# Four gather slots and six weight buffers in place of five and four, in a two-layer decoder trunk

## The chip, the cores and the metric

The kernel runs on 1 core of one Trainium2 chip. The metric is the device time of one launch in microseconds (us); lower is better.

## The reference

Two layers of a decoder trunk in float32, for 256 prompt rows and 32 sample rows (8 sequences of 4). The model width is 1024.

```python
for l in range(2):
    h = rmsnorm(x) @ w_in[l]                   # 1024 -> 8192: u, v, GLU, q, three gates
    y_a = spatial_gate(gelu(u), gelu(v))       # chunks of 128, 8 groups
    y_b = silu(layernorm(conv31(glu)))         # causal depthwise conv, 31 taps
    y_m = mem_attend(q, mem_k, mem_v)          # 4 heads, 256 memory tokens; sample rows: per-sequence caches
    x += (sig(gA)*(y_a@w_o_a) + sig(gB)*(y_b@w_o_b) + sig(gM)*(y_m@w_o_m)) @ w_out
    x += peer(rmsnorm(x))
# peer: per token and each of 8 heads, top 16 of 16384 experts through product keys;
#   hid = gelu(x . u_tab[eid]);  y = sum over the 128 experts of gate * hid * v_tab[eid]
y = rmsnorm(x)
```

The expert part fetches, for each of 288 tokens and 2 layers, 128 rows of the u table and 128 rows of the v table by index.

## The kernel before

The work is cut into four portions m = 0 to 3, two to a layer: an even portion has the first 128 prompt rows, an odd one the other 128 prompt rows and the 32 sample rows. A portion is first mixed (everything up to the expert keys, `mixing(m)` on each engine) and then has its experts retrieved. Retrieval of portion m runs beside the mixing of portion m+1: each engine has one program order that alternates a unit of retrieval with the slice of mixing that `reach` allows after it. Portion 0 is mixed alone at the start (to about 300 us), portion 3 is retrieved alone at the end.

**Retrieval.** Its unit is the pair, t = 0 to 287: two indirect gathers, each of 128 rows of 8 KB (a u row and its v row side by side), so 2 MB to a pair. Eight pairs are a step (32 tokens, 4 heads), k = t % 8 is the pair's place in its step; two steps are a group. The queues do this for pair t:

- POOL: `gather(t)` (L359), both gathers, after it has waited until the values of pair t - SLOTS are done (`v_used`). There are SLOTS = 5 slots of two 1 MB buffers.
- DVE: `dots(t)` (L972), the two dot products with the u halves, 1.22 us each.
- ACT: one Gelu of two columns (L422, `gel`).
- DVE: work for later steps that is put between the dots and the diags of some pairs: the top-16 search of one half (`pick_half`, at k = 0 and k = 7), `pick_pairs` at k = 1, `pick_experts` at k = 2, `gates` at k = 4. Then `diags(t)` (L983).
- PE: `values(t)` (L1358), 8 matmuls with the v halves; its end is `v_used`.
- DVE: at k = 1 of every even step also `add_group` (L991), behind the diags.

**Weights and caches.** SP loads 264 pieces, nearly all 1 MB, in the one order of `ITEMS` into a ring of RING = 4 buffers; piece n waits until piece n - RING is used up. The order in an odd portion is glu 8, q 4, ck 8 (K cache of the eight sequences), va 4, cv 8 (V cache), mg 8, ua 4, mg 16, out 4, ffn, wq 4, keys; an even one has mk 4 and mv 4 behind glu and no ck and cv. PE reads them in that order: L1057 and L1063 the weights, L1207 the ck pieces, L1236 the cv pieces.

SP's program holds other transfers between the loads, with waits of their own, and what comes behind such a wait is not issued before it ends:

```python
if (kind, i) == (("va", 3), ("ck", 3))[p]:            # p = m % 2
    sp.wait_ge(S["pe_o"], at("pe_o", m, 4))           # the prompt rows' attention is done
    sp.wait_ge(kv_stored, 32 * (l + 1))
    sp.dma_start(phase[:, 2 * D:4 * D], rows_in[rows_l, :])    # L329
```

In the same way an odd portion has, ahead of its fifth piece (glu 4), a wait for the transposes at the start of that portion (L312 and the loads behind it), and both kinds have a wait for the spatial gate's LayerNorm behind mg 5 (L332).

The buffers take 2 x 5 x 8 KB and 4 x 8 KB of each partition, 112 KB in all.

Of the kernel before, what the change touches and what calls it, by code (L numbers as in the profile page):

```python
# [35 lines left out]
FIRST = [sum(STEPS[i % 2] for i in range(m)) for m in range(PORTIONS + 1)]  # L36
NSTEP = FIRST[PORTIONS]
PAIRS = 8
SLOTS = 5
SCORE_SLOTS = 10  # L40


# [17 lines left out]

ITEMS = [it for m in range(PORTIONS) for it in items(m)]
ITEM = {it: n for n, it in enumerate(ITEMS)}
RING = 4
WKIND = [("glu", 8), ("mk", 4), ("mv", 4), ("q", 4), ("va", 4), ("ua", 4), ("mg", 24), ("out", 4), ("wq", 4)]
WROW = {}
for _k, _c in WKIND:
# [27 lines left out]
def freed(m, kind, i):  # L94

    nt = len(TB[m % 2])
    name, k = {"glu": ("pe_glu", 2 * i + 2), "mk": ("pe_mk", 2 * i + 2), "mv": ("pe_mv", 2 * i + 2), "q": ("pe_q", 2 * i + 2),
               "ck": ("pe_sk", i + 1), "va": ("pe_va", nt * (i + 1)), "cv": ("pe_so", i + 1), "mg": ("pe_mg", 2 * i + 2),
               "ua": ("pe_ua", 2 * i + 2), "out": ("pe_out", nt * (i + 1)), "ffn": ("xfrow", nt), "wq": ("pe_wq", 2 * i + 2),
               "keys": ("pe_sc", STEPS[m % 2])}[kind]  # L100
    return name, at(name, m, k)
# [49 lines left out]
def build(nc, x_in, consts_in, mem_in, cache_in, state_in, w_in, small_in, rows_in, ffn_in, fing_in, ws_in, wss_in, bs_in,  # L151
          keys_in, uv_in, y_out, memk_out, memv_out, convp_out, convs_out, vn_out):
    with ExitStack() as ctx:
        def sb(name, shape, dt=F32):
            return ctx.enter_context(nc.sbuf_tensor(name, shape, dt))

        def sem(name):
            return ctx.enter_context(nc.semaphore(name))

        S = {name: sem("s_" + name) for name in tuple(PER) + RUN}  # L160
        w_landed = [sem(f"w_landed{i}") for i in range(RING)]
        uv_landed = [sem(f"uv_landed{i}") for i in range(SLOTS)]
        x_landed = [sem(f"x_landed{t}") for t in range(TILES)]
# [5 lines left out]

        uv_region = sb("uv", [P, 2 * SLOTS * 2 * D])  # L170
        uvbuf = [uv_region[:, 2 * D * i:2 * D * (i + 1)] for i in range(2 * SLOTS)]
        ring_region = sb("ring", [P, RING * 2 * D])
        ring = [ring_region[:, 2 * D * i:2 * D * (i + 1)] for i in range(RING)]

# [84 lines left out]
        def landed(m, kind, i):  # L259
            n = ITEM[m, kind, i]  # L260
            return w_landed[n % RING], 16 * (n // RING + 1)

        def buf(m, kind, i):
            return ring[ITEM[m, kind, i] % RING]

        @block.sync
        def _(sp):
            def load(m, kind, i):
                n = ITEM[m, kind, i]
                l = m // 2  # L270
                if n >= RING:
                    name, k = freed(*ITEMS[n - RING])
# [78 lines left out]
        def _(pool):  # L351
            def gather(t):
                s, k, b = t // PAIRS, t % PAIRS, t % SLOTS
                pool.wait_ge(S["ids"], s + 1)
                if t >= SLOTS:
                    pool.wait_ge(S["v_used"], t - SLOTS + 1)
                for i in range(2):
                    c = 16 * (s % 2) + 2 * k + i
                    nc.gpsimd.indirect_dma_start(  # L359
                        out=uvbuf[2 * b + i], out_offset=None, in_=uv_in,  # L360
                        in_offset=bass.IndirectOffsetOnAxis(ap=ids[:, c:c + 1], axis=0),
                    ).then_inc(uv_landed[b], 16)
# [1098 lines left out]
```

## Time and profile before

| what | value |
|---|---|
| median of 3 runs | 2566.31 us (2560.45 to 2570.62) |
| the profiled execution: time, span | 2567.09 us, 2564.9 us |
| busy share: PE, DVE, ACT, POOL | 75%, 66%, 25%, 26% |
| mean granted TensorE clock | 0.855 |
| bytes moved by DMA | 905.88 MB, mean 353 GB/s |
| of these, gathers and SP's queue | 604.02 MB and 299.90 MB |
| gathers, ring pieces | 576 and 264 |

How to read it: busy shares are means over stretches with different limits, so the windows (busy time of each engine, granted clock, share of time in which the 16 DMA engines were busy, GB/s) have to be read beside them. The span is that of one execution; the time of the same execution is 2.2 us longer.

### The profile page before, as it was taken

How to read it: one execution, taken by the hardware profiler on the slowest of the kernel's cores; microseconds unless marked ns; L12 is line 12 of the kernel's file. 1: busy time of each engine (PE TensorE's matmuls, PEld its weight loads, DVE VectorE, ACT ScalarE, POOL GpSimd, SP SyncE). 2: the span in 40 equal slices, each digit the busy share in tenths (PEclk: the TensorE clock that was granted, in tenths of full speed). 3: DMA queues.
4: the chain of work that ended last, by engine and by line, in shares of the span. 5: the costliest groups of instructions: out<-in, count | busy, mean ns of one | idle time of the engine just before them, and what ended most of it. 6: DMA issues, size and time to landing. Idle time of an engine off the chain costs nothing.

```text
span 2564.9 us, 31043 instructions
## 1 busy us (share of the span) xinstructions
PE 1936.3 (75%) x10696; PEld 1213.1 (47%) x10696; DVE 1684.3 (66%) x4711; ACT 648.4 (25%) x1185; POOL 661.8 (26%) x608
## 2 busy tenths in 40 slices
PE   8999767577989758977889757757898975545554
PEld 7889636235766406644557404523676641000010
DVE  4372257867645586788765675787664478888785
ACT  2112232122142314122334213211214231131110
POOL 0000031212222332323222342122311234443442
PEclk9999979788899969988899877878889987687767
DMA  7566699689789899999899999878878989999997
GB/s 269 198 247 223 254 407 366 253 341 383 294 328 370 349 422 402 407 416 368 340 421 415 421 421 388 333 293 341 352 289 329 368 318 422 421 420 420 411 410 299
DMA packets 127835, 905.88 MB, mean 353 GB/s; under 512 B 16112, under 2 KB 16576, under 8 KB 18368
## 3 DMA queue, kind: packets, MB, share of 16 engines
q0 software_dynamic: 82944, 604.02, 58.5%
q1 hardware_dynamic: 44736, 299.90, 30.0%
q8 instruction: 85, 1.39, 0.2%
q14 instruction: 70, 0.57, 0.1%
HBM read 895.75 MB, written 8.11 MB: 352 GB/s over the span
## 4 chain that ended last, share of the span: by engine, by line
PE 49%; DVE 21%; DMA 17%; issue 5%; DVEq 3%; ACT 3%; POOL 3%; POOLq 0%; ACTq 0%
PE bank L1057 25%; DMA uv<-uv_in,idx_u 13%; PE bank L1358 11%; PE bank L1063 8%; DVE uv L972 6%; DVE yB L671 3%; POOL uv L359 2%; DMA ring<-w_in 2%; DVE diag L983 2%; DMA ring<-cache_in 2%; DVE tmp_s L681 1%; DVE yB L686 1%; ACT L422 1%; DVEq L666 1%; DVE pick L943 1%
## 5 line engine op out<-in xcount | busy, mean ns | idle before, releaser
L1358 PE MATMUL bank<-uv,diag 128*32 128x512 f32 x2304 | 728.5, 766 | 473.7 <-DVE diag L983 464.6
L359 POOL DMA_INDIRECT uv<-uv_in,idx_u x576 | 617.8, 1073 | 1709.4 <-PE bank L1358 1419.0
L972 DVE CUSTOM_DVE_ANT_0 uv<-uv,xrep 128x1024 f32<-128x1024 f32 x576 | 681.8, 1221 | 112.9 <-DMA uv<-uv_in,idx_u 112.4
L1358 PEld LDWEIGHTS bank<-uv,diag 128*32 128x32 f32 x2304 | 134.8, 128 | 936.4 <-DVE diag L983 637.5
L1057 PEld LDWEIGHTS bank<-xnT,ring 128*128 128x128 f32 x4096 | 531.9, 196 | 94.9 <-issue 88.0
L1057 PE MATMUL bank<-xnT,ring 128*128 128x128 f32 (+1 forms) x4096 | 556.7, 295 | 10.7 <-ACT yMA L422 8.6
L422 ACT ACTIVATE pick<-pick 128x2 f32<-128x2 f32 (+1 forms) x324 | 69.6, 215 | 1152.5 <-DVE pick L972 1151.9
L422 ACT ACT_TABLE_LOAD x255 | 327.2, 1283 | 15.1 <-PE bank L1063 6.0
L671 DVE SCALAR_TENSOR_TENSOR yB<-ext_p,small,yB 128x128 f32<-128x128 f32 x960 | 282.8, 356 | 20.5 <-issue 1.4
L983 DVE TENSOR_SCALAR diag<-consts,pick 128x32 f32<-128x32 f32 x576 | 151.1, 317 | 63.0 <-ACT pick L422 57.4
L1057 PE MATMUL bank<-yMA,ring 128*128 128x128 f32 (+1 forms) x1024 | 137.2, 287 | 0.0
L1057 PEld LDWEIGHTS bank<-yMA,ring 128*128 128x128 f32 x1024 | 131.1, 191 | 0.0
L853 DVE TENSOR_TENSOR sg<-sg,bank 128x128 f32<-128x128 f32 (+1 forms) x64 | 19.5, 304 | 166.7 <-PE bank L1057 127.6
L422 ACT ACTIVATE sg<-bank 128x160 f32<-128x160 f32 (+1 forms) x128 | 36.8, 290 | 211.9 <-PE bank L1057 211.3
L1063 PE MATMUL bank<-ring,xnT 128*128 128x256 f32 (+1 forms) x384 | 88.9, 389 | 1.6 <-DMA ring<-w_in 1.0
L422 ACT ACTIVATE phase<-bank 128x256 f32<-128x256 f32 (+2 forms) x88 | 30.6, 348 | 227.3 <-PE bank L1063 116.0
L1063 PE MATMUL bank<-ring,merged 128*128 128x256 f32 (+1 forms) x384 | 87.0, 383 | 0.8 <-DVE merged L855 0.8
L1063 PEld LDWEIGHTS bank<-ring,xnT 128*128 128x128 f32 (+1 forms) x384 | 62.6, 167 | 31.5 <-issue 10.2
L1063 PEld LDWEIGHTS bank<-ring,merged 128*128 128x128 f32 (+1 forms) x384 | 61.1, 163 | 30.7 <-issue 12.9
L731 DVE TENSOR_TENSOR ext_p<-bank,sg 128x128 f32<-128x128 f32 x32 | 9.3, 291 | 95.4 <-PE bank L1057 95.4
L1057 PE MATMUL bank<-yB,ring 128*128 128x128 f32 (+1 forms) x512 | 68.6, 287 | 0.0
L612 ACT ACTIVATE xrep<-xnf 32x1024 f32<-32x1024 f32 x64 | 67.4, 1053 | 1.5
(151 smaller groups left out, 1470.6 us busy)
## 6 DMA issues: line engine op xcount, KB each, us to landing
ring<-w_in SPq DMA_DIRECT2D x224, 1024.0 KB, 8.8
ring<-cache_in SPq DMA_DIRECT2D x32, 1024.0 KB, 11.6
uv<-uv_in,idx_u POOLq DMA_INDIRECT x576, 12.6
phase<-rows_in SPq DMA_DIRECT2D x4, 1024.0 KB, 6.8
ring<-keys_in SPq DMA_DIRECT2D x4, 1024.0 KB, 8.9
ext_s<-state_in SPq DMA_DIRECT2D x2, 1088.0 KB, 11.0
convs_out<-ext_s SPq DMA_DIRECT2D x2, 1088.0 KB, 16.3
ext_s<-mem_in SPq DMA_DIRECT2D x2, 1024.0 KB, 14.7
```

The lines of the kernel that those rows point to most:

```text
L359: nc.gpsimd.indirect_dma_start(out=uvbuf[2 * b + i], out_offset=None, in_=uv_in, in_offset=bass.IndirectOffsetOnAxis(ap=ids[:, c:c + 1], a ...
L422: ins = nc.scalar.activation(out, in_, func, bias=bias, scale=scale, **({} if accum is None else {"accum_out": accum}))
L612: ins = nc.scalar.activation(xrep[gg % 2][32 * i:32 * (i + 1), :], xnf[1 if t == 2 else 0][r0:r0 + 32], ACT.Copy)
L666: dve.drain()
L671: ins = V.scalar_tensor_tensor(out=yB[:, c, 0:P], in0=ext_p[:, c, w:w + P], scalar=wconv[:, c, w:w + 1], in1=yB[:, c, 0:P], op0=ALU.mult, ...
L681: V.tensor_tensor(tmp_s[:, :, :, :], ext_s[:, :, :, w:w + DSEQ], wide, ALU.mult)
L686: ins = V.tensor_tensor(ys, tmp_s[:, :, :, :], ys, ALU.add)
L972: ins = V.tensor_tensor_reduce(out=u, in0=u, in1=xrep[gg % 2][:, :], scale=1.0, scalar=0.0, op0=ALU.mult, op1=ALU.add, accum_out=hid[:, c: ...
L983: ins = V.tensor_scalar(diag[:, t % 4, i], fold, gel[:, c:c + 1], gate[:, c:c + 1], ALU.mult, ALU.mult)
L1057: ins = MM(out, w[:, k, P * b:P * (b + 1)], rhs(k), start=k == 0, stop=k == KB - 1)
L1063: ins = MM(out, lhs(k), w[:, k, :], start=k == 0, stop=k == KB - 1)
L1358: ins = MM(vbank[gg % 2][32 * n:32 * (n + 1), :], diag[:, t % 4, i], uvbuf[2 * b + i][:, D + 512 * n:D + 512 * (n + 1)], start=first and i ...
```

## The change

SLOTS goes from 5 to 4, RING from 4 to 6. A slot has two buffers, so gathers have 8 buffers and ring pieces 6, and the sum stays at 14 buffers of 8 KB a partition. All waits that are counted from SLOTS and RING follow; no instruction is added, removed or put elsewhere in a queue. `gather(t + SLOTS)` stays where it was in POOL's program, so at each place it now fetches the pair one earlier.

```diff
-SLOTS = 5
+SLOTS = 4
...
-RING = 4
+RING = 6
```

## Rows read from the trace of the kernel before

**Rows 1.** The page, part 2: DMA busy tenths in 40 slices of 64 us.

```profile
DMA  7566699689789899999899999878878989999997
```

**Rows 2.** Waits, whole span: who for whom, us in total, times, longest.

```profile
POOL uv L359 <- PE bank L1358: 1419.0, 244, 18.3
...
DVE uv L972 <- DMA uv<-uv_in,idx_u: 112.4, 77, 7.4
...
PE bank L1207 <- DMA ring<-cache_in: 27.7, 7, 6.3
...
PE bank L1236 <- DMA ring<-cache_in: 14.0, 6, 3.7
```

**Rows 3.** Windows: length, busy PE PEld DVE ACT POOL, clock, DMA share, GB/s.

```profile
2064.00:2096.00 32.00, 31.23 (x246) 21.36 (x244) 22.12 (x63) 10.72 (x28) 11.54 (x10) 1.00 0.80 310
...
2112.00:2496.00 384.00, 209.35 (x602) 37.11 (x604) 312.04 (x831) 69.41 (x141) 163.02 (x150) 0.73 1.01 419
816.00:864.00 48.00, 41.12 (x202) 24.41 (x201) 27.25 (x72) 8.44 (x19) 10.11 (x10) 0.89 0.80 299
864.00:960.00 96.00, 58.78 (x283) 18.79 (x281) 69.08 (x186) 21.39 (x48) 37.48 (x34) 0.79 1.01 421
...
1280.00:1560.00 280.00, 208.37 (x1190) 118.02 (x1188) 184.83 (x500) 88.39 (x155) 88.08 (x83) 0.87 1.01 420
...
556.00:571.00 15.00, 5.69 (x28) 1.55 (x32) 14.18 (x36) 5.04 (x8) 3.55 (x4) 0.69 0.60 220
```

**Rows 4.** Timeline of PE, cv pieces of portion 1: start, us.

```profile
574.67 1.03 PE L1236 MATMUL bank<-ring,ext_s 128*32 128x256 f32 x12
578.20 1.56 PE L1236 MATMUL bank<-ring,ext_s 128*32 128x256 f32 x16 [2.50 <-DMA ring<-cache_in]
...
582.68 3.29 PE L1358 MATMUL bank<-uv,diag 128*32 128x512 f32 x8
585.97 1.07 PE L1236 MATMUL bank<-ring,ext_s 128*32 128x256 f32 x16
...
592.76 3.35 PE L1358 MATMUL bank<-uv,diag 128*32 128x512 f32 x8
596.04 2.44 PE L1057 MATMUL bank<-xnT,ring 128*128 128x160 f32 x16
...
622.30 3.63 PE L1358 MATMUL bank<-uv,diag 128*32 128x512 f32 x8 [6.57 <-DVE diag L983]
```

**Rows 5.** Timeline of PE, cv pieces of portion 3.

```profile
1782.53 1.03 PE L1236 MATMUL bank<-ring,ext_s 128*32 128x256 f32 x12
...
1801.37 2.44 PE L1057 MATMUL bank<-xnT,ring 128*128 128x160 f32 x16
```

**Rows 6.** Timeline of SP, at the ck pieces of portion 1.

```profile
487.94 0.33 SPq L329 DMA_DIRECT2D phase<-rows_in  x1
488.97 4.63 SPq L281 DMA_DIRECT2D ring<-cache_in  x4
```

**Rows 7.** Timelines of DVE and POOL in the last retrieval, from several windows.

```profile
2193.14 1.22 DVE L972 CUSTOM_DVE_ANT_0 uv<-uv,xrep 128x1024 f32<-128x1024 f32 x1 [0.49 <-DMA uv<-uv_in,idx_u]
...
2209.85 1.67 POOL L359 DMA_INDIRECT uv<-uv_in,idx_u  x1 [4.15 <-PE bank L1358]
...
2213.02 1.23 DVE L972 CUSTOM_DVE_ANT_0 uv<-uv,xrep 128x1024 f32<-128x1024 f32 x1 [1.25 <-DMA uv<-uv_in,idx_u]
...
2217.97 1.23 DVE L972 CUSTOM_DVE_ANT_0 uv<-uv,xrep 128x1024 f32<-128x1024 f32 x1 [1.67 <-DMA uv<-uv_in,idx_u]
...
2233.83 1.22 DVE L972 CUSTOM_DVE_ANT_0 uv<-uv,xrep 128x1024 f32<-128x1024 f32 x1 [1.32 <-DMA uv<-uv_in,idx_u]
...
2252.09 1.70 POOL L359 DMA_INDIRECT uv<-uv_in,idx_u  x1 [4.93 <-PE bank L1358]
```

**Rows 8.** POOL's gathers of 1848 to 1852 us, one pair, no other gather under way.

```profile
L359 POOL DMA_INDIRECT uv<-uv_in,idx_u x2: 933/934/936, 1850.2 to 1851.4; - x2
...
DMA to landing us min/median/max: 5.6/6.6/7.5
```

## The prediction

> **What bounds the kernel now.** I began with the page's DMA row [rows 1]. For most of the run the DMA engines are eight or nine tenths busy, but there are sevens and eights between, so neither transfers nor an engine bound all of it. Both kinds of buffer that change can bind only where somebody waits for what lands in them, so the waits came next [rows 2]. POOL waits 1419 us for PE, which means that the slots are nearly always full: that costs nothing as long as what has landed lies ready. Waits that do cost are few. DVE waits for gathered rows 112 us in 77 places, PE for ring pieces 27.7 us at the ck pieces (L1207) and 14.0 us at the cv pieces (L1236), in both odd portions together; for weights it hardly waits at all.
>
> The windows say where [rows 3]. In the last retrieval the DMA engines are full: 1.01 at 419 GB/s for 384 us, with PE busy 209 and DVE 312 of them. The same holds at the end of retrieval 0 (864 to 960 us) and for 280 us of retrieval 1. Before two of these stretches the engines had room: 0.80 at 816 to 864 and 0.80 at 2064 to 2096. So there are two regimes. Beside a mixing, PE and DVE set the pace and pieces of the ring can be late in bursts; once a mixing is done, a retrieval is bound by the pace at which pairs land.
>
> **The ring, 4 to 6.** Work out the cv place of portion 1 [rows 4]. PE has used cv 3 at 574.67 + 1.03 = 575.7, waits 2.50 us for cv 4, more for cv 5 and cv 7, and begins mg 0 at 596.04: 20.3 us. Its work in these is four pieces at 1.07, two values at 3.29 and 3.35, and two transposes with the wait ahead of them, 1.2 us: 12.1 us. From 556 to 571 the DMA engines were only 0.60 busy [rows 3], because PE stood on DVE and POOL and all buffers were full. Six buffers take in cv 4 and cv 5 there. The pieces behind them then take the places in the queue that cv 4 to cv 6 had: cv 6 is there at 578.2, when cv 4 was, and mg 0 by 586.0, when cv 6 was. The work of 12.1 us ends at 587.8, behind both, so mg 0 begins there: 8.2 us saved. In portion 3 the same stretch takes from 1783.56 to 1801.37, 17.8 us [rows 5]; with the same work 5.7 us are saved. Together 13.9 us. After these places PE's slice of mixing is what DVE waits for, so I let the gain stand to the end of each mixing.
>
> At the ck place nothing is gained, although the waits are twice as long. SP stands at L329 behind ck 3 until 487.94, with two empty buffers under the change; then come the rows_in transfer and ck 4 to ck 7 from 488.97 [rows 6]. Now ck 4 would be issued some 0.7 us sooner, but behind the same rows_in, in the same queue, at the same share of full engines. Between 0 and 1 us; I take 0. If SP's wait were not there, it would be up to 27.7 us [rows 2]. The opening (portion 0 alone) has no ring wait either: 0. Other transfers of SP, behind its waits at glu 4, L329 and L332, are tied to other engines' work and keep their times, plus the shift.
>
> **The slots, 5 to 4, beside a mixing.** A gather is issued when a slot comes free, as before, so the traffic is the same at the same times, but it carries the pair one earlier: every pair lands one pair's turn later than it did. There DVE takes up a pair about every 9 us (64 of them from some 330 to 900 us) and hardly waits for a gather, so what has landed covers it. Without that cover it would cost a turn once, about 9 us. I take 0.
>
> **The slots in the three stretches that gathers bound.** The pace is one pair in 4.95 us (2213.02 to 2217.97) [rows 7], which is 2.1 MB at 419 GB/s [rows 3].
>
> *Entry.* Where such a stretch begins with all slots full, one pair less has landed, and it must be fetched at full engines: 5 us once. At 864 and at 2096 us the engines had had room before, so the two ring pieces that were fetched instead don't make up for it: SP keeps two pieces further ahead through retrieval 0's end, and at the last one nothing follows. 5 us each. In retrieval 1 the engines are full from 1280 on, and there the ring brings its 2 MB into the stretch and stops at glu 3 of portion 3 as before (the wait ahead of glu 4), so it asks for 2 MB less within it. These cancel: 0, with 5 as the bound.
>
> *Round trips.* With four slots the gather that POOL issues when pair t is done is pair t+4. The tight one is k = 2, behind pick_pairs and pick_experts. In an odd step, pair k = 1 is taken up at 2193.14 and the gather behind pair k = 2 is issued at 2209.85: 16.7 us. It must now bring the pair that is due five paces after k = 1, 24.8 us, so it has 8.1 us to land. In an even step add_group lies between as well: 2233.83 to 2252.09 is 18.3 us, which leaves 6.5 us [rows 7]. A pair alone lands 8.7 us after its first issue (1851.4 + 7.5 less 1850.2) [rows 8]. So the stream slips by 0.6 us in an odd step and 2.2 in an even one. The other pairs of a step have the room: they come free 5 to 10 us after they land, of four paces' 19.8. The last retrieval has about four odd and five even such steps with picking: 4 x 0.6 + 5 x 2.2 = 13.4 us. Retrieval 0's end has one odd step, 0.6; retrieval 1's end I put at 2.
>
> The landing time under the change is the unknown. Its lower bound is the first gather of the lone pair, 5.6, plus the 1.2 us between the two issues, as if only the bytes counted: 6.8, and then the slips are 0 and 0.3, 1.5 us in all. Its upper bound adds a slow issue (1.67 against 0.93 us, rows 7 and 8) to each half: 10.2, slips of 2.1 and 3.7, 27 us. I take 8.7, since it is the same transfer with nothing ahead, and nothing ahead is what a late issue means.
>
> **Sum.** Entry 10.0, last retrieval 13.4, ends of retrievals 0 and 1 2.6, ring -13.9: +12.1 us. The profiled execution took 2567.1 us, 0.8 above the median of three, so 2579.2 on its scale and 2578.4 against the median. I say 2578 us. No change, within 0.5% (about what a measurement of this kernel can tell), is 2553.5 to 2579.1, so my number lies just inside its edge.
>
> **The rivals.**
>
> - *The round trips hide.* If a pair that is issued while the one before it still moves lands in the 6.8 us of the lower bound, only the entries cost: 10.0 + 1.5 + 1 - 13.9 = -1.4, 2565 us. For it: in the dense stretches most of a gather's time is queueing. Against it: lone pairs take 8.7 in every case that I looked at, and an overlap of 2 us would have to come from somewhere. The Trainium skill's page "DMA: Bandwidth & Descriptors", section "Anatomy of one DMA — SWDGE (gpsimd) path", fits a transfer as about 2.0 us plus its bytes at 436 GB/s; as an estimate that is 6.8 us for a pair's 2.1 MB and speaks for this rival, while the trace's lone pair takes 8.7, and the measurement decides.
> - *The ring gain is given back.* Some 10 us behind each cv place PE stands 6.57 us for DVE's diag [rows 4]. If DVE is late there for reasons of its own (picks beside POOL's LayerNorm), the earlier PE only waits longer. Then +26.0: 2592 us. Against it: DVE's slices ahead of that diag wait for mg 0 and mg 1 themselves.
> - *The ring gains at ck too, on the other side.* If gathers with a slot less leave the engines to SP's queue behind 488 us, ck 4 to ck 7 and va 0 land as fast as PE takes them, and the 27.7 us go as well: -15.6, 2551 us. It decides once ck 4 lands as soon as PE is through with ck 3, a few us behind 488.97 [rows 6]. Against it: gathers are issued at the same moments with four slots as with five.
>
> **Chances.** My forecast 0.58, its own range 2569 to 2588, half of it on each side of 2579; hidden round trips 0.16; gain given back 0.14; gain at ck 0.12. Faster by over 0.5% (below 2553.5) comes from the last and a little of the first rival: 0.13. Within 0.5%: 0.29 + 0.15: 0.44. Slower: 0.29 + 0.14: 0.43. The range leaves out most of the ck case and the upper end of the costliest trips: 2554 to 2595.
>
> **What would show it.** In the profile after, the cv row of PE's waits (14.0) should fall to a few us and the ck row (27.7) stay; mg 0 of portion 1 should begin 6 to 9 us sooner. In the last retrieval the DMA share should fall below 1, to about 0.97, at some 406 GB/s, with DVE's waits for uv up in the pairs behind k = 2, above all in even steps; the stretch from 2112 us on should be 18 us longer. At the ends of retrievals 0 and 1 the DMA share stays near 1. I am wrong if the last retrieval keeps 419 GB/s (first rival), if PE's longer waits for the diag eat the cv gain (second), or if the ck waits shrink (third). A starved gather beside a mixing, with DVE waiting for uv there, would be a cost that I have not counted.

## The result and the profile after

The kernel with four slots and six ring buffers took 2576.64 us (median of 20 runs, 2566.11 to 2586.43), the kernel before 2564.27 us beside it (20 runs, 2556.35 to 2573.69). The ratio is 1.0056, 95% interval 1.0044 to 1.0068: slower by 12.4 us in the medians, 14 us by the ratio.

The profiled execution of after took 2570.7 us, 6 below its median; that of before lies 3 above its own. So the two traces differ by 3.4 us of span where the medians differ by 12.4, and a place by place account has to find the other 9 us as luck of these two executions. It does, further down.

The page of after: the span, the DMA busy tenths in 40 slices (before: [rows 1]), the uv queue's bytes and DVE's dots.

```profile
span 2568.3 us, 31044 instructions
...
DMA  7476598699889999988999999779988789999997
...
q0 software_dynamic: 82944, 604.02, 58.4%
...
L972 DVE CUSTOM_DVE_ANT_0 uv<-uv,xrep 128x1024 f32<-128x1024 f32 x576 | 681.9, 1221 | 146.1 <-DMA uv<-uv_in,idx_u 145.4
```

The waits of after over the whole span, which answer to [rows 2].

```profile
POOL uv L359 <- PE bank L1358: 1456.1, 246, 18.3
...
DVE uv L972 <- DMA uv<-uv_in,idx_u: 145.4, 80, 7.5
...
PE bank L1207 <- DMA ring<-cache_in: 26.5, 7, 6.3
...
PE bank L1236 <- DMA ring<-cache_in: 0.7, 1, 0.7
```

The two kinds of buffer show in two rows. The wait for cv pieces is gone (14.0 to 0.7), that for ck pieces is as it was (27.7 and 26.5), and DVE waits 33 us longer for gathered rows, in about as many places: the single waits got longer.

Windows of after, the same stretches as in [rows 3] where they answer to them (length, busy PE, PEld, DVE, ACT, POOL, granted clock, DMA share, GB/s).

```profile
864.00:960.00 96.00, 51.05 (x212) 9.94 (x203) 65.19 (x177) 21.32 (x45) 36.92 (x33) 0.75 1.00 410
...
1280.00:1560.00 280.00, 208.66 (x1173) 116.39 (x1171) 184.11 (x497) 88.24 (x154) 86.53 (x82) 0.87 1.00 412
...
2112.00:2496.00 384.00, 211.37 (x580) 36.80 (x578) 297.34 (x793) 65.83 (x134) 158.14 (x144) 0.69 0.98 398
...
571.00:608.00 37.00, 30.43 (x250) 21.95 (x240) 32.35 (x78) 9.30 (x16) 18.82 (x12) 0.99 1.01 413
```

The last retrieval is the plain one: 419 GB/s before, 398 now, over the same 384 us of the clock; its gathers are the same in number and size, so they take longer. The last row is the stretch of the last cv pieces of portion 1 and of mg behind them; in the kernel before it read as follows.

```profile
571.00:608.00 37.00, 29.17 (x219) 16.13 (x212) 22.02 (x76) 4.52 (x9) 6.02 (x7) 0.85 1.00 411
```

PE's timeline of after at the cv pieces of portion 1, which answers to [rows 4].

```profile
578.87 1.07 PE L1236 MATMUL bank<-ring,ext_s 128*32 128x256 f32 x16 [0.75 <-DMA ring<-cache_in]
...
580.80 1.91 PE L1358 MATMUL bank<-uv,diag 128*32 128x512 f32 x8
583.12 2.44 PE L1057 MATMUL bank<-xnT,ring 128*128 128x160 f32 x16 [0.41 <-DMA ring<-w_in]
```

mg 0 begins at 583.12 in place of 596.04. In portion 3 it begins at 1789.59 in place of 1801.37 [rows 5]:

```profile
1789.59 2.44 PE L1057 MATMUL bank<-xnT,ring 128*128 128x160 f32 x16
```

How a slip looks. DVE's dots of after in an even step of the last retrieval (two rows are a pair; those shown are first halves, but for the one at 2425.66), and then POOL's gathers of the same step.

```profile
2396.04 1.23 DVE L972 CUSTOM_DVE_ANT_0 uv<-uv,xrep 128x1024 f32<-128x1024 f32 x1 [0.38 <-DMA uv<-uv_in,idx_u]
...
2403.78 1.23 DVE L972 CUSTOM_DVE_ANT_0 uv<-uv,xrep 128x1024 f32<-128x1024 f32 x1
...
2416.59 1.23 DVE L972 CUSTOM_DVE_ANT_0 uv<-uv,xrep 128x1024 f32<-128x1024 f32 x1 [0.32 <-DMA uv<-uv_in,idx_u]
...
2424.51 1.23 DVE L972 CUSTOM_DVE_ANT_0 uv<-uv,xrep 128x1024 f32<-128x1024 f32 x1 [4.64 <-DMA uv<-uv_in,idx_u]
2425.66 1.22 DVE L972 CUSTOM_DVE_ANT_0 uv<-uv,xrep 128x1024 f32<-128x1024 f32 x1
2429.47 1.22 DVE L972 CUSTOM_DVE_ANT_0 uv<-uv,xrep 128x1024 f32<-128x1024 f32 x1 [1.80 <-DMA uv<-uv_in,idx_u]
```

```profile
2406.32 0.94 POOL L359 DMA_INDIRECT uv<-uv_in,idx_u  x1 [3.98 <-PE bank L1358]
...
2414.23 1.80 POOL L359 DMA_INDIRECT uv<-uv_in,idx_u  x1 [5.57 <-PE bank L1358]
2416.34 0.94 POOL L359 DMA_INDIRECT uv<-uv_in,idx_u  x1 [0.31 <-issue]
```

Pair k = 1 is taken up at 2396.04. The gather behind pair k = 2 goes out at 2414.23, 18.2 us later (18.3 in the kernel before [rows 7]), and it carries pair k = 6. Pairs 5, 6 and 7 are taken up at 2416.59, 2424.51 and 2429.47: 7.9 us and then 4.96. One gap of 7.9 where the pace is 4.95 is a slip of 3.0 us, and DVE's wait in it is 4.64 where the other waits of the step are under 2. Behind it the pairs come at the pace again, and the 3.0 us stay.

Both traces can be laid over each other by the starts of the dots, pair by pair. After less before, in us, and what changed over each stretch (an ordinary table, worked out from the L972 rows):

```
place                                     difference   change
opening                                       -1.9      -1.9
cv place of portion 1                        -12.2     -10.3
entry into retrieval 0's end                  -7.5      +4.6
its odd step (+1.6), and just behind (+0.6)   -5.3      +2.2
beside the mixing of portion 2, 1100-1115     -2.0      +3.3
retrieval 1's end (+4.8 on the way)           -1.9      +0.1
cv place of portion 3                        -12.2     -10.3
the mixing behind it                         -18.9      -6.7
entry into the last retrieval                -13.8      +5.1
slips of the last retrieval                   +3.8     +17.6
```

Two changes have no edit behind them: the opening's -1.9, where both kernels issue the same work, and the -6.7 behind the second cv place, where PE's granted clock was 0.81 in the kernel before and 0.90 after over the same 84 us (1820 to 1904). Without these two the table sums to +12.3, the medians' +12.4. The opening is luck of the execution of before: wide54 below, which is the kernel before in everything but the last retrieval, starts its dots 1.5 us ahead of it too. That the -6.7 is luck as well is shown only in part, and the table of places at the end of the experiments says how far. So the agreement to 0.1 us is closer than this account can carry.

### The profile page after: what moved, and what is told of

Read it like the earlier page. It is cut to its first block, busy times and chain, and to the rows that moved or that the text cites. A ratio compares the mean times of both kernels' runs of the same rounds, so it can differ in the third digit from the quotient of the medians.

```text
span 2568.3 us, 31044 instructions
## 1 busy us (share of the span) xinstructions
PE 1935.0 (75%) x10696; PEld 1208.8 (47%) x10696; DVE 1682.8 (66%) x4711; ACT 648.5 (25%) x1185; POOL 666.2 (26%) x608
## 4 chain that ended last, share of the span: by engine, by line
PE 49%; DVE 21%; DMA 16%; issue 5%; DVEq 3%; ACT 3%; POOL 3%; POOLq 0%; ACTq 0%
PE bank L1057 25%; DMA uv<-uv_in,idx_u 13%; PE bank L1358 12%; PE bank L1063 8%; DVE uv L972 7%; DVE yB L671 3%; DMA ring<-w_in 3%; POOL uv L359 3%; DVE diag L983 2%; DVE tmp_s L681 1%; DVE yB L686 1%; ACT L422 1%; DVEq L666 1%; DVE pick L943 1%; PE bank L1288 1%
## 5 line engine op out<-in xcount | busy, mean ns | idle before, releaser
L1358 PE MATMUL bank<-uv,diag 128*32 128x512 f32 x2304 | 737.8, 775 | 495.4 <-DVE diag L983 486.7
L972 DVE CUSTOM_DVE_ANT_0 uv<-uv,xrep 128x1024 f32<-128x1024 f32 x576 | 681.9, 1221 | 146.1 <-DMA uv<-uv_in,idx_u 145.4
## 6 DMA issues: line engine op xcount, KB each, us to landing
ring<-cache_in SPq DMA_DIRECT2D x32, 1024.0 KB, 17.6
uv<-uv_in,idx_u POOLq DMA_INDIRECT x576, 10.4
```

The source lines that it names most:

```text
L972: ins = V.tensor_tensor_reduce(out=u, in0=u, in1=xrep[gg % 2][:, :], scale=1.0, scalar=0.0, op0=ALU.mult, op1=ALU.add, accum_out=hid[:, c: ...
L1358: ins = MM(vbank[gg % 2][32 * n:32 * (n + 1), :], diag[:, t % 4, i], uvbuf[2 * b + i][:, D + 512 * n:D + 512 * (n + 1)], start=first and i ...
```

## The experiments

The theory to be tested: the change is a gain from the ring at the cv places (about 20 us in both portions), and a loss from the slots, most of it round trips in the last retrieval (about 16 to 18 us) besides the entries (about 10). The rivals: the loss lies elsewhere, the ring gave little, or the ck place stays because of memory traffic and not because of SP's order. All ratios are to the kernel before, whose median was 2565.3 us beside s4r4, hold46, ck46 and wide46 and 2565.8 us beside the other four (23 runs each). s4r4 was run 4 times, hold46, s4r5 and wideck46 6 times, the others 12 times.

**s4r4: the slots alone.** Four slots, and the ring as it was.

```diff
-SLOTS = 5
+SLOTS = 4
```

> Slots alone: 4 slots, 4 ring buffers, so the loss without the ring's gain. My theory, with the sizes of the changed kernel's profile: about 33 us for the slots (entry of retrieval 0's end 4.6, its even step 2.2, a starved gather in the mixing beside retrieval 1 3.3, last retrieval 22.7) and 5 more, since the ring no longer makes up for the entry of retrieval 1's end: 38 us, ratio to the kernel before 1.0145. Rival, the ring gives nothing and the slots cost all of the 12 us that were measured: 1.005.

Measured: 2601.6 us, ratio 1.0135 (1.0118 to 1.0153). The slot costs some 35 us, and from there to after's 1.0056 the ring gives back 0.0079, 20 us. For four slots with four ring buffers the prediction's terms make 31 us: 26.0, and the 5 us that it let the ring cancel at the end of retrieval 1. That term is real (+4.1 here, about 0 in after), so the ring's 20 us stand against 13.9 + 5. The slots were put 4 us too low and the ring 1 us. PE's wait at the cv pieces is back, and the last retrieval reads as in after:

```profile
PE bank L1236 <- DMA ring<-cache_in: 16.8, 8, 3.9
```

```profile
2112.00:2496.00 384.00, 209.94 (x578) 36.10 (x576) 295.48 (x788) 67.93 (x136) 160.99 (x147) 0.71 0.98 397
```

**hold46: four slots, six ring buffers, but cache pieces come no earlier than with four.** SP waits for the item four before, for ck and cv pieces only.

```diff
-                    name, k = freed(*ITEMS[n - RING])
+                    name, k = freed(*ITEMS[n - (4 if kind in ("ck", "cv") else RING)])
```

> 4 slots, 6 ring buffers, but a ck or cv piece is loaded only when the piece four before it is used, as with four buffers; all other pieces keep the six. My theory: the ring's whole gain is at the cv pieces, two times some 10 us, so this is 20 us above the changed kernel, ratio 1.0135, and PE's wait for cv pieces (L1236) is back at 14 us. Rival, the two further buffers help by running ahead everywhere: then it stays near the changed kernel's 1.0056, cv waits or not.

Measured: 2597.7 us, 1.0126 (1.0106 to 1.0146). The weights' greater lead is worth next to nothing (1.0126 against 1.0135, inside the intervals). Of the ring's gain, 0.0070 (18 us) hangs on cache pieces that come early; the prediction had 13.9 for these. The wait for cv pieces stands where it stood before:

```profile
PE bank L1207 <- DMA ring<-cache_in: 28.9, 8, 6.5
...
PE bank L1236 <- DMA ring<-cache_in: 14.3, 6, 3.7
```

**s4r5: four slots, five ring buffers.**

```diff
-SLOTS = 5
+SLOTS = 4
...
-RING = 4
+RING = 5
```

> 4 slots and 5 ring buffers. My theory: one cv piece more is taken in while the engines stand, worth about 5 us in each of the two odd portions, so half the ring's gain: between 1.0135 (4 and 4) and 1.0056 (4 and 6), at 1.0095. Rival, the second piece gives nothing more, since PE is held by its own work by then: 1.0060 or less.

Measured: 2588.6 us, 1.0092 (1.0076 to 1.0108). So the first further ring buffer gives 0.0043 and the second 0.0036. The wait for cv pieces is halved (6.8 us), which fits: each buffer takes in one more piece ahead of PE's burst.

**ck46: SP's wait at L329 two pieces later.** The transfer of rows_in, with the wait ahead of it, goes behind ck 5 in place of ck 3 in odd portions.

```diff
-                    if (kind, i) == (("va", 3), ("ck", 3))[p]:
+                    if (kind, i) == (("va", 3), ("ck", 5))[p]:
```

> The changed kernel with SP's wait for the attention and the rows_in load behind ck 5 in place of ck 3 in the odd portions. My theory: that wait, not the ring's size, kept the two further buffers empty while the DMA engines stood idle; ck 4 and ck 5 land early, ck 6 to va 0 each take a place two pieces sooner, some 10 us in each odd portion: 20 us below the changed kernel, ratio 0.998, PE's wait at L1207 down from 26.5 to under 15 us. Rival: other engines are as late there, and the ratio stays at 1.0056.

Measured: 2568.5 us, 1.0006 (0.9991 to 1.0021). Against after's 1.0056 that is a gain of 0.0050, 13 us. The cause is shown: in after, SP stood ahead of L329 with two empty buffers and then issued four ck pieces at once; here six ck pieces are out beforehand. SP's timeline of after, and then that of ck46:

```profile
485.99 0.33 SPq L329 DMA_DIRECT2D phase<-rows_in  x1
486.36 2.08 SPq L281 DMA_DIRECT2D ring<-cache_in  x4
```

```profile
407.63 25.87 SPq L281 DMA_DIRECT2D ring<-cache_in  x6
485.98 0.33 SPq L329 DMA_DIRECT2D phase<-rows_in  x1
487.01 1.42 SPq L281 DMA_DIRECT2D ring<-cache_in  x2
```

```profile
PE bank L1207 <- DMA ring<-cache_in: 5.3, 2, 2.9
```

The wait falls by 21 us, the time by 13; 20 us and a ratio of 0.998 had been expected. The expectation counted nearly the whole wait as time; in the trace each ck place became only some 7 us shorter (7.5 and 6.9), since PE then stands for DVE's diag in part of the gaps that the cache pieces had filled: from 480 to 571 us its waits for ck pieces go from 14.2 to 2.4 us and those for the diag from 8.6 to 13.3.

**late46: in the last retrieval, add_group comes behind pair k = 5 and no longer behind k = 1.** It takes two adds (1.37 us together) out of the way of the late gather, in even steps alone.

```diff
-                    if k == 1 and s % 2 == 0 and s:
+                    if k == (5 if m == PORTIONS - 1 else 1) and s % 2 == 0 and s:
```

> The changed kernel, but in the last retrieval add_group of the even steps goes from behind pair k = 1 to behind pair k = 5. My theory: an even step's slip (some 3 us in the changed kernel's profile, an odd one's 1.3) is the round trip behind k = 2 with add_group's 1.4 us in it; without it the even steps slip as the odd ones do, five times 1.4 to 1.7 us less: 7 to 8 us below the changed kernel, ratio 1.0025 to 1.003. Rival, the slips come from the gathers' side (a late issue, a slower transfer) and not from DVE's order: ratio stays at 1.0056.

Measured: 2572.0 us, 1.0029 (1.0014 to 1.0045), a gain of 0.0027 or 7 us over about five even steps, 1.4 us in each. The stretch has part of its rate back, 404 GB/s. A few lines of one engine that move no byte give back half of what the whole change lost: the slips are round trips and no loss of bandwidth.

```profile
2112.00:2496.00 384.00, 214.14 (x592) 36.46 (x592) 302.65 (x808) 69.19 (x140) 161.28 (x146) 0.73 0.99 404
```

**wide46: from pair 208 on, the six ring buffers serve as three further slots.** The last retrieval has no mixing beside it, so the ring lies idle there.

```diff
+WIDE = SLOTS + RING // 2
+T0 = -(-PAIRS * FIRST[PORTIONS - 1] // SLOTS) * SLOTS
+def slot(t):
+    return t % SLOTS if t < T0 else (t - T0) % WIDE
...
+        uvbuf += ring[0:2 * (WIDE - SLOTS)]
...
+                if t >= T0 + WIDE:
+                    pool.wait_ge(S["v_used"], t - WIDE + 1)
+                elif t >= T0 + SLOTS:
+                    pool.wait_ge(S["pe_sc"], at("pe_sc", PORTIONS, 0))
...
+                    if t == T0:
+                        for a in range(T0 + SLOTS, T0 + WIDE):
+                            gather(a)
```

> The changed kernel, but from pair 208 on the last retrieval also uses the ring's six buffers, free by then, as three further slots: 7 in all. My theory: of the last retrieval's 22.7 us the entry (5) stays, since it lies ahead of pair 208, and the slips behind k = 2 (about 16) go: DMA share back at 1.01, ratio about 0.9995. Rival, the last retrieval is slower because gathers issued later or in other buffers move at a lower rate: then it stays at 1.0056 and the DMA share below 1.

Measured: 2563.1 us, 0.9995 (0.9983 to 1.0007). With seven slots in that stretch alone 0.0061 comes back, 15.6 us; the slips behind pair 208 in the trace of after were 16.4 us. The rate is that of the kernel before:

```profile
2112.00:2496.00 384.00, 210.35 (x606) 37.68 (x608) 308.62 (x818) 68.77 (x141) 170.14 (x158) 0.73 1.01 420
```

**wide54: the same seven slots in the kernel before** (five, and two out of four ring buffers, from pair 210 on).

```diff
-SLOTS = 4
+SLOTS = 5
...
-RING = 6
+RING = 4
```

> The kernel before (5 slots, 4 ring buffers), but from pair 210 on with the ring's four buffers as two further slots, 7 in all. My theory: with five slots the last retrieval already runs at the transfers' pace (419 GB/s), so nothing changes: ratio 1.000 within 0.2%. Rival, more slots always help a little (the round trips behind k = 2 cost something at five as well): 0.996 or less.

Measured: 2565.6 us, 0.9997 (0.9985 to 1.0010). Five slots had already covered the round trip: a sixth and a seventh gain nothing. This is the control for wide46. Its gain is the loss undone, and no gain of its own.

**wideck46: both remedies.** Four slots and six ring buffers, the wide last retrieval, and rows_in behind ck 5.

```diff
-                    if (kind, i) == (("va", 3), ("ck", 3))[p]:
+                    if (kind, i) == (("va", 3), ("ck", 5))[p]:
```

> The two remedies together: 4 slots and 6 ring buffers, SP's rows_in load behind ck 5, and 7 slots from pair 208 on. My theory: the gains lie in different stretches and add: 0.9995 for the wide last retrieval less the 0.0050 that the ck place gave gives 0.9945, about 14 us below the kernel before. Rival, the DMA engines have no room for both: above 0.998.

Measured: 2552.7 us, 0.9945 (0.9928 to 0.9962). It beats both kernels, the one before by 13 us in the medians and 14 by the ratio. The two remedies add up: 0.9995 less the 0.0050 of ck46 is 0.9945. It is the version to keep.

Not tried: five slots together with five or six ring buffers.

**The places in the traces of these runs.** Each column is one execution, laid over before as in the table above: by how much its dots shifted against before over each stretch, in us (an ordinary table, worked out from the rows of the dots). wide46 and late46 are after's program up to the last retrieval, wide54 is before's.

| place (pairs) | after | wide46 | late46 | s4r4 | hold46 | wide54 |
|---|---|---|---|---|---|---|
| opening (to pair 0) | -1.9 | -1.8 | -2.9 | +1.7 | -1.8 | -1.5 |
| cv place of portion 1 and behind (25 to 32) | -10.2 | -7.0 | -10.0 | +6.5 | 0.0 | -1.3 |
| beside the mixing of portion 2 (86 to 92) | +3.1 | +3.0 | +3.3 | 0.0 | +3.5 | 0.0 |
| retrieval 1's end (124 to 150) | 0.0 | +0.1 | 0.0 | +4.1 | +0.1 | -2.3 |
| cv place of portion 3 (169 to 170) | -10.3 | -10.2 | -9.0 | +1.6 | +1.8 | +3.5 |
| the mixing behind it (170 to 176) | -6.8 | -4.1 | -2.0 | -6.5 | -6.7 | -1.9 |
| last retrieval (208 to 287) | +16.4 | +0.6 | +8.4 | +19.2 | +18.3 | -0.8 |

The gain at the cv places, 7 us or more at each, is there in the three executions that may use all six ring buffers for cache pieces, and in none of the others. Behind the second one the same program moved by 6.8, 4.1 and 2.0 us, so part of after's -6.7 is its execution; but s4r4 and hold46, which have no gain from the ring there, moved as far, so the ring does not make it, and what the four-slot kernels have in common there stays open. So does the +6.5 of s4r4 in portion 1, which hold46 lacks.

## Why the prediction was right in its sum, and by which steps

The forecast was +12.1 us and 2578 us; measured were +12.4 and 2576.6. The direction, the two mechanisms and their places held. Two terms of opposite sign were too small, one was missing, and they offset one another, so that the number came out within 1.4 us is in part luck:

```
term                                 forecast   in the profile
cv places, both portions              -13.9        -20.6
ck places                               0            0
beside a mixing                         0           +3.3
ends of retrievals 0 and 1, entry      +5.0         +4.6
their slips                            +2.6         +2.3
entry into the last retrieval          +5.0         +5.1
slips of the last retrieval           +13.4        +17.6
sum                                   +12.1        +12.3
```

*The ring at cv.* The mechanism held: two pieces land early, the ones behind move up in the queue. The size was off by 6.7 us, and the step that failed is "12.1 us of work". It took the work at the durations of before. With the pieces there, PE ran almost without gaps, at a granted clock of 0.99 between 571 and 608 us in place of 0.85, that is, nearly all of it at the 2.4 GHz level: two pairs' values took 1.9 us each where they had taken 3.29 and 3.35 [rows 4]. Together that is 2.8 us, the size of the gap between the 8.2 that had been forecast and the 11.0 by which mg 0 began sooner once the opening's shift is taken off (the trace's dots moved by 10.3). That it goes with the waits is seen in wide46, the same program up to there. Its execution happened to wait 3.5 us for the last cv piece, and the values behind that wait took 3.59 us:

```profile
578.54 1.07 PE L1260 MATMUL bank<-ring,ext_s 128*32 128x256 f32 x16 [3.48 <-DMA ring<-cache_in]
...
580.47 3.59 PE L1382 MATMUL bank<-uv,diag 128*32 128x512 f32 x8
584.00 2.44 PE L1081 MATMUL bank<-xnT,ring 128*128 128x160 f32 x16
```

In portion 3 the dots moved by 10.3 for 5.7. By hold46 the gain at cv is 18 us in both portions together, so the forecast was 4 us too small by the runs and 6.7 by this one trace. The 20 us of s4r4 are another sum: they hold the 4 us at retrieval 1's end as well, and the 3 us that the mixing of portion 2 costs (below) are taken off.

*The ck places.* Right, with its cause: SP's wait, which ck46 moved. The bound of 27.7 us without that wait was not reached; the gain of ck46 was 13.

*Beside a mixing.* The prediction named the cover (pairs lie ready) and the price of losing it (a turn of 9 us). The cover did run out at one place, which the prediction's last sentence named as a cost that it had not counted. Near 1094 us SP stores memk_out and memv_out and loads three weights behind them, at full engines. The two pairs issued there take 16.9 and 23.6 us to land, in place of 10 to 13. SP's and DVE's timelines of after:

```profile
1093.81 0.34 SPq L324 DMA_DIRECT2D memk_out<-phase  x1
1094.20 0.43 SPq L325 DMA_DIRECT2D memv_out<-phase  x1
1094.67 9.90 SPq L284 DMA_DIRECT2D ring<-w_in  x3
```

```profile
1112.85 1.23 DVE L972 CUSTOM_DVE_ANT_0 uv<-uv,xrep 128x1024 f32<-128x1024 f32 x1 [3.75 <-DMA uv<-uv_in,idx_u]
...
1122.76 1.23 DVE L972 CUSTOM_DVE_ANT_0 uv<-uv,xrep 128x1024 f32<-128x1024 f32 x1 [0.53 <-DMA uv<-uv_in,idx_u]
```

In the kernel before, with landings of 19 and 21 us at the same stores, the pairs were ready 10 us ahead and DVE did not wait. The loss needs both halves of the change. All traces with four slots and five or six ring buffers show it (3.0 to 3.9 us), s4r4's does not: with four ring buffers SP came to the stores only at 1119.1, 5 us behind the gathers of the pair (1113.9), where in after it was there 2 us ahead of them (1093.8 and 1095.9).

*The entries.* Measured 4.6 and 5.1 for 5 each. The slips of retrieval 0's end came at k = 6 of its odd step, as written down, 1.6 us for the forecast 0.6, with 0.6 behind it. Retrieval 1's end was written down as cancelling, and did: +4.8 on the way, 0 at its end. That it is the ring that cancels is shown: with four ring buffers (s4r4) 4.1 us stay.

*The last retrieval's slips.* Right in place (behind k = 2, larger in even steps), too small: 2.3 to 4.0 us in each of five even steps for the forecast 2.2, and 0.2 to 2.1 in each of four odd ones for 0.6; some 5 us of it are returned where the kernel before had small gaps of its own, which leaves 17.6.

The times from taking up k = 1 to the late issue were as read (16.5 to 17.0 and 18.0 to 18.3 us). The step that failed is the landing time of 8.7 us, "the same transfer with nothing ahead": the late pairs land 9.1 to 10.4 us after their first issue, 9.7 in the mean, by when DVE, which waits for them, takes them up. The larger part of that extra microsecond is the issue on POOL and not what is ahead. POOL's first issue took 1.64 to 1.97 us in nine of the ten steps where the lone pair's took 0.93 [rows 8], so the second goes out 2.0 us behind the first and not 1.2 (2414.23 and 2416.34 above). From the second issue on they land after 7.1 to 8.2 us, 7.7 in the mean, against 7.5 for the lone pair. So 0.7 us comes from the slow issue and 0.2 from the rest, the pair ahead among it, which lands 1.6 to 4.0 us after the late issue; in s4r4 and ck46, whose traces have the landings themselves, it is 0.6 to 0.7 and 0.5 to 0.6. The slow issue stood in the rows: it is the same place of POOL's program that took 1.67 and 1.70 us in the kernel before [rows 7], and the prediction had it in its upper bound only.

The Trainium skill's page "DMA: Bandwidth & Descriptors", section "Anatomy of one DMA — SWDGE (gpsimd) path", would give 6.8 us for these bytes by its fit, as an estimate; the trace does not agree, for these pairs (9.1 to 10.4) even less than for the lone one (8.7).

*The rivals.* Hidden round trips: fell, since the rate did drop to 398 GB/s and wide46 gives back 0.0061. Gain given back: fell, since PE's waits for diag between 571 and 700 us are the same in both traces (11.8 us, 3 times, longest 6.6). Gain at ck too: fell, 26.5 us stayed. Of the signs promised, the cv wait, the ck wait, the DMA share (0.98 for 0.97) and the longer last retrieval (22.7 us for 18.4, entry included) came as said; mg 0 came 11 us sooner for 6 to 9, and its rate was 398 for 406 GB/s.

Open: why POOL's first issue is slow at that place, before and after; and what of the -6.7 us behind the second cv place is luck.

## What to carry to other kernels

To weigh one buffer against another, ask for each stretch what it hides: slots hide a round trip (from taking up a pair to the landing of the one that replaces it, over the pace times the slots), ring pieces hide a burst, and the same memory can be the one kind in one stretch and the other in the next. Before a further buffer is bought, see whether the queue that should fill it stands in a wait of its own: moving one transfer behind two others was worth 13 us here, about two thirds of what the two ring buffers gave at cv.

## What the hardware showed that was not expected

- Four slots of 2.1 MB pairs kept the engines at 398 GB/s, five and seven at 419 to 421: above the round trip further slots gained nothing (wide54).
- The late gather pairs of the last retrieval take 9.1 to 10.4 us to land, one alone 8.7. The larger part of it is POOL's first issue of the two, mostly 1.64 to 1.97 us in place of 0.93; the pair ahead, still moving for 1.6 to 4.0 us, is behind 0.6 us of it at most.
- PE's gaps cost more than their length. Where no wait for a cv piece was over 0.8 us (after, late46, ck46), the eight matmuls of the values just ahead of mg 0 in portion 1 took 1.91 us; behind a wait of 2.3 to 3.9 us (before, wide54, wide46, s4r5, s4r4) they took 3.1 to 3.6 us. The granted clock over 571 to 608 us was 0.99 in after and 0.85 in before; in wide54, the kernel before in that stretch, it was 0.91, so part of that difference is the execution.
